# Groups of two picks instead of four in an expert retrieval, v rows added two groups behind

## The reference, cut to what matters

```python
def block(args):
    xb, eb, gb = args
    a = jnp.einsum('td,thkd->thk', xb, u_tab[eb])
    coef = gb.astype(xb.dtype) * jax.nn.gelu(a)
    return jnp.einsum('thk,thkd->td', coef, v_tab[eb])
```

## Time and profile before

| | us |
|---|---|
| median of 3 runs | 2582.67 (2576.73 to 2587.87) |
| the profiled execution | 2576.18 |
| its span, first to last instruction | 2574.3 |
| PE, DVE, ACT, POOL busy | 1894.1, 1692.0, 550.0, 1521.5 |
| HBM read | 936.55 MB, 365 GB/s over the span |

### The profile page before, as it was taken

How to read it: one execution, slowest core, us unless ns; L and a number is a source line. 1 busy time by engine, 2 the same in 40 slices (tenths; PEclk the granted TensorE clock), 3 DMA queues, 4 the chain that set the end, 5 groups by cost and what they waited for, 6 DMA issues and landing times.

```text
span 2574.3 us, 19294 instructions
## 1 busy us (share of the span) xinstructions
PE 1894.1 (74%) x5226; PEld 836.3 (32%) x5226; DVE 1692.0 (66%) x3756; ACT 550.0 (21%) x1369; POOL 1521.5 (59%) x1562
## 2 busy tenths in 40 slices
PE   6779776686777555686677678677777777777776
PEld 3444343352232212343332234335322222222222
DVE  0337876776899555557779657577968886554444
ACT  1432323221122001212222112222211111111111
POOL 2005554666677545566656655466667777677774
PEclk8879987898999767798889988788989999999999
DMA  9918987999999999999899999789999999999997
GB/s 340 347 60 310 405 326 250 382 367 403 386 408 408 402 394 373 341 369 406 327 404 387 366 378 396 284 300 384 360 374 409 409 409 409 373 410 410 409 409 319
DMA packets 295970, 939.88 MB, mean 365 GB/s; under 512 B 30692, under 2 KB 44360, under 8 KB 295864
## 3 DMA queue, kind: packets, MB, share of 16 engines
q0 software_dynamic: 222496, 809.28, 80.9%
q1 hardware_dynamic: 71304, 127.38, 13.5%
q10 hardware_dynamic: 2064, 2.00, 0.2%
HBM read 936.55 MB, written 2.00 MB: 365 GB/s over the span
## 4 chain that ended last, share of the span: by engine, by line
DMA 27%; DVE 23%; PE 20%; POOL 13%; issue 8%; ACT 4%; SPq 1%; DVEq 0%; ACTq 0%; POOLq 0%
DMA vbuf<-in_peer_v_dram,eidx 11%; DVE ubuf L2143 10%; DMA ubuf<-in_peer_u_dram,eidx 10%; PE ysum L1234 7%; POOL vbuf L2200 6%; POOL ubuf L2200 6%; PE bank L948 4%; DMA wring<-in_w_mod_dram 3%; DVE acc L2136 2%; PE bank L1200 2%; PE bank L1167 2%; DMA wring<-in_w_in_dram 1%; SPq L844 1%; DVE scratch L2017 1%; DVE scratch L2019 1%
## 5 line engine op out<-in xcount | busy, mean ns | idle before, releaser
L1234 PE MATMUL ysum<-vbuf,diag 128*128 128x512 f32 x2356 | 1212.9, 649 | 354.3 <-DMA vbuf<-in_peer_v_dram,eidx 253.6
L2143 DVE CUSTOM_DVE_ANT_0 ubuf<-ubuf,h_bank 128x1024 f32<-128x1024 f32 x768 | 910.5, 1219 | 386.4 <-DMA ubuf<-in_peer_u_dram,eidx 358.9
L2200 POOL DMA_INDIRECT ubuf<-in_peer_u_dram,eidx x768 | 737.1, 960 | 601.4 <-DVE dot L2143 245.4
L2200 POOL DMA_INDIRECT vbuf<-in_peer_v_dram,eidx x768 | 771.1, 1004 | 402.6 <-issue 189.9
L1234 PEld LDWEIGHTS ysum<-vbuf,diag 128*128 128x128 f32 x2356 | 440.9, 203 | 1077.9 <-DMA vbuf<-in_peer_v_dram,eidx 585.1
L1620 ACT ACTIVATE act_dot<-dot 128x4 f32<-128x4 f32 x192 | 39.4, 205 | 1259.4 <-DVE dot L2143 1257.9
L2136 DVE SCALAR_TENSOR_TENSOR acc<-vbuf,coef,acc 128x1024 f32<-128x1024 f32 x173 | 222.1, 1284 | 68.4 <-DMA vbuf<-in_peer_v_dram,eidx 56.9
L1631 ACT ACTIVATE diag<-ident,coef 128x128 f32<-128x128 f32 x589 | 201.1, 393 | 255.7 <-DVE coef L2148 203.7
L948 PE MATMUL bank<-wring,hT 128*128 128x512 f32 (+1 forms) x416 | 191.5, 618 | 21.7 <-DMA wring<-in_w_in_dram 12.5
L948 PEld LDWEIGHTS bank<-wring,hT 128*128 128x128 f32 x416 | 84.6, 206 | 124.4 <-issue 98.4
L891 PE MATMUL bank<-wring,cond 128*32 128x512 f32 x288 | 51.8, 855 | 56.8 <-DMA wring<-in_w_mod_dram 50.7
(11 more groups left out here) (287 smaller groups left out, 1332.9 us busy)
## 6 DMA issues: line engine op xcount, KB each, us to landing
wring<-in_w_mod_dram SPq DMA_DIRECT2D x19, 2048.0 KB, 19.4
wring<-in_w_in_dram SPq DMA_DIRECT2D x11, 2048.0 KB, 19.6
wring<-in_w_out_dram SPq DMA_DIRECT2D x7, 2048.0 KB, 19.7
wring<-in_peer_w_q_dram SPq DMA_DIRECT2D x7, 2048.0 KB, 18.9
ubuf<-in_peer_u_dram,eidx POOLq DMA_INDIRECT x768, 9.1
vbuf<-in_peer_v_dram,eidx POOLq DMA_INDIRECT x768, 9.1
wring<-in_w_in_dram SPq DMA_DIRECT2D x4, 1664.0 KB, 16.7
ubuf<-in_w_mod_dram SPq DMA_DIRECT2D x3, 2048.0 KB, 14.4
```

Of the source, the lines that this page charges most:

```text
L1234: mm = pe.matmul(ysum[:, b, :], diag[:, (n - 1) % DIAGS, :], vbuf[:, pick % V_SLOTS, 512 * b:512 * b + 512], start=first and r == rows[0], ...
L2143: dve.tensor_tensor_reduce(ubuf[:, n % U_SLOTS, :], ubuf[:, n % U_SLOTS, :], h2_bank[:, :, :].rearrange("p b n -> p (b n)"), 1.0, 0.0, ALU ...
L2200: pool.indirect_dma_start(buf[:, n % slots, :], None, rows, bass.IndirectOffsetOnAxis(eidx[:, t % 2, p:p + 1], 0))\
```

## The change

Groups have two picks (`G = 2`, so `NG` = 64). The v rows of group i are added beside group i + 2 (`LAG`), on PE and on DVE; a tile ends with two groups of rows. `coef` has three buffers in place of two, as a group's coefficients are still read while the next two are written. The slots of u and v stay at six. The planner's constants for four picks are halved, and its tail is 4 groups in place of 2; the last two groups of a tile have one row of two on DVE.

```diff
-G = 4
-U_SLOTS = G + 2
-V_SLOTS = G + 2
+G = 2
+LAG = 2
+U_SLOTS = 6
+V_SLOTS = 6
-TAIL = 2
+TAIL = 4
-ROW_US, ADD_US, DOTS_US = 2.1, 1.3, 5.4
+ROW_US, ADD_US, DOTS_US = 2.1, 1.3, 2.7
-PACE_US = 9.6
+PACE_US = 4.8
...
     for what, i, *more in schedule():
         if what == "groups":
-            if more[0]:
-                share[i, more[0] - 1] = shares(pe, dve)[1]
+            if more[0] >= LAG:
+                share[i, more[0] - LAG] = shares(pe, dve)[1]
             if more[1] == NG:
-                share[i, more[0]] = 1
+                for k in range(NG - LAG, NG):
+                    share[i, k] = 1
...
-        coef = sb("coef", [P, 2, G])
+        coef = sb("coef", [P, LAG + 1, G])
...
-                if lo <= 1 < hi:
+                if lo <= LAG < hi:
                     if t:
 
                         pe.wait_ge(y_taken, nth("y_taken", t - 1))
                     group(0, True, False)
-                for i in range(max(lo - 1, 1), hi - 1):
+                for i in range(max(lo - LAG, 1), hi - LAG):
                     group(i, False, False)
                 if hi == NG:
-                    group(NG - 1, False, True)
+                    for i in range(NG - LAG, NG):
+                        group(i, False, i == NG - 1)
...
-                    if i:
-                        add_rows(i - 1)
+                    if i >= LAG:
+                        add_rows(i - LAG)
                     dve.wait_ge(gelu_done, NG * t + i + 1)
-                    dve.tensor_tensor(coef[:, i % 2, :], act_dot[:, :], gates[:, t % 2, G * i:G * i + G], ALU.mult).then_inc(coef_done, 1)
+                    dve.tensor_tensor(coef[:, i % (LAG + 1), :], act_dot[:, :], gates[:, t % 2, G * i:G * i + G], ALU.mult).then_inc(coef_done, 1)
...
                 if hi == NG:
-                    add_rows(NG - 1)
+                    for i in range(NG - LAG, NG):
+                        add_rows(i)
...
                 fetch_u(n)
-                if n >= G:
-                    fetch_v(n - G)
-            for n in range(total - G, total):
+                if n >= G * LAG:
+                    fetch_v(n - G * LAG)
+            for n in range(total - G * LAG, total):
                 fetch_v(n)
```

More of the change, by code:

```diff
@@ L1630, in group @@
                             act.wait_ge(v_free, n - DIAGS)
-                        act.activation(diag[:, (n - 1) % DIAGS, :], ident[:, :], ACT.Copy, scale=coef[:, i % 2, r:r + 1]).then_inc(diag_built, 1)
+                        act.activation(diag[:, (n - 1) % DIAGS, :], ident[:, :], ACT.Copy, scale=coef[:, i % (LAG + 1), r:r + 1]).then_inc(diag_built, 1)
                 if lo == 0:
@@ L2132, in add_rows @@
                         if vector_rows(n) - 1 == (vector_rows(PICKS * t - 1) if t else 0):
-                            dve.tensor_scalar(acc[:, :], vbuf[:, n % V_SLOTS, :], coef[:, i % 2, r:r + 1], None, ALU.mult).then_inc(v_added, 1)
+                            dve.tensor_scalar(acc[:, :], vbuf[:, n % V_SLOTS, :], coef[:, i % (LAG + 1), r:r + 1], None, ALU.mult).then_inc(v_added, 1)
                         else:
                             dve.wait_ge(v_added, vector_rows(n) - 1)
-                            dve.scalar_tensor_tensor(out=acc[:, :], in0=vbuf[:, n % V_SLOTS, :], scalar=coef[:, i % 2, r:r + 1], in1=acc[:, :],
+                            dve.scalar_tensor_tensor(out=acc[:, :], in0=vbuf[:, n % V_SLOTS, :], scalar=coef[:, i % (LAG + 1), r:r + 1], in1=acc[:, :],
                                                      op0=ALU.mult, op1=ALU.add).then_inc(v_added, 1)
```

## The result

The changed kernel takes 2574.0 us (median of 19 runs, 2569.6 to 2580.9), the kernel before 2583.9 us beside it (19 runs, 2576.7 to 2590.7). The ratio is 0.9970, with a 95% interval of 0.9961 to 0.9978: about 8 us faster (the two medians differ by 9.9). The forecast was 2608, slower; the range held the time. The profiled execution took 2573.6 us (before 2576.2), so the two profiles themselves differ by less than the medians do, and a reading by stretches can explain the larger shifts within the kernel, not the last few microseconds of the whole.

The account below looks back on a forecast made before the run. DMA bytes were taken to bound the kernel wherever no engine holds picks back. The terms 8 + 11 + 5 + 4 + 5 - 8 gave +25 us, 2601 from the profile's 2576.2; 2608 as median of runs, range 2545 to 2645.

Parts of the forecast that it names:

- What bounds the kernel: Whole kernel: DMA bytes at 410 GB/s wherever no engine holds picks back; 105 us in tiles 0 to 3 winnable.
- Twice the handovers: 192 more gelu and coef handovers, 0.43 us each, cost where DVE sets the pace: +8 us, bounds 0 and 82.
- table loads: ACT: about 10 more table switches at 1.30 us, 13 us, of which 5 show: +5 us (0 to 13).
- Packing of tile 1: Tile 1's top-k: denser gaps make three halves 18 us too long, cushion takes about 7: +11 us.
- Packing of tile 2: Tile 2's top-k: level near 8.2, 3.2 us a pick instead of 3.0, 7 us less the cushion: +5 us.
- Who adds v rows: Projections of tiles 2 and 3: 29 rows move from DVE to PE, mostly covered by DMA: +4 us, bounds 0 and 60.
- Finer interleaving: Two attention stretches: scores come earlier behind two rows than four; -4 us each, -8 in all, bounds -32 and +6 a stretch.
- The lag: Fetch order and lag: POOL's sequence stays the same, and the third coefficient buffer only makes the lag legal: 0 us.
- rival B: Faster: finer PE and DVE alternation shortens attention stretches and starved places, -35 us, 2548; attention share over 0.8 decides; 28%.
- Boundaries: Five tile starts: the last two groups' DVE rows of 1.28 us lie within DVE's 9.9 us wait: 0 (0 to 7).
- the signs for a wrong prediction: Wrong if tile 1 isn't longer, or if tiles 0 and 3 are each over 10 us shorter.
- A: The forecast itself: DVE and PE get tighter, coarser gaps; 2590 to 2640, attention share 0.66 to 0.75; 50%.

Follow-up runs that it names:

- a_places: The changed kernel's groups of two and lag of two, but beats dealt by four picks as in the kernel before, 179 rows on DVE; 2597.3 us, 1.0055.
- f_pairs: The changed kernel with tile 1's modulation beats planned at 3.0 and 0.8 us, so two share a gap; 2557.6 us, 0.9897.
- a_cap: a_places with at most two of four rows on DVE, 133 instead of 179, spread over both pairs; 2586.1 us, 1.0022.
- s_split: a_places with each gap's beats shared between its two pairs, still 179 rows on DVE; 2573.9 us, 0.9968.
- m_dve: The kernel before (groups of four, lag one) with each gap's beats cut in two on DVE alone; 2560.9 us, 0.9913.
- c_lag1: The changed kernel with a lag of one group instead of two, 146 rows on DVE instead of 152; 2572.9 us, 0.9972.
- f_mid: f_pairs with each gap's beats cut in two, a dot behind each half, on PE too; 2545.9 us, 0.9867.
- end0: The changed kernel with no row on DVE in a tile's last two groups, instead of one each; 2566.1 us, 0.9939.
- best: The changed kernel with the edits of f_pairs and end0, and layer 1's constants and keys requested earlier; 2555.9 us, 0.9906.
- m_two: The kernel before with each gap's beats cut in two on DVE, and PE's four rows put between the halves; 2591.9 us, 1.0041.

## Why the prediction was wrong, step by step

**What bounds the kernel** stood. Bytes set the time wherever no engine holds the picks back, POOL has no margin to catch up, and all that moved was time lost against 409 GB/s.

**Twice the handovers, +8, and table loads, +5.** a_places has the handovers with the lag, and the table loads of before (35): 14 us where I had 8. So the handovers, with the lag, were sized too low. The gelu waits were forecast at 2 x 59 and came to 190.8 us, since a gelu queued behind a beat on ACT waits with it. Table loads rose by 8 in the changed kernel, forecast about 10; no run has them by themselves. A load with the activation behind it, in its timeline of ACT:

```profile
1032.28 0.40 ACT L1634 ACTIVATE diag<-ident,coef 128x128 f32<-128x128 f32 x1 [0.23 <-DVE coef L2151]
1032.70 1.28 ACT L1333 ACT_TABLE_LOAD   x1
1034.00 0.52 ACT L1333 ACTIVATE decay<-decay 128x384 f32<-128x384 f32 x1
```

It takes 1.3 us with both sides of it. The drain of 1.38 us that the Trainium skill (ScalarE: Activation LUTs, What ACT_TABLE_LOAD costs) adds doesn't show here either.

**Packing of tile 1, +11.** The mechanism was right and the half searches were as worked out, 56.6 us for 20 picks against 57.3 (64 picks in the 181 us above). The cushion was not: I took 7 of 18 us off for what is queued, and tile 1 got 17 us longer, its ledger 0.2 to 16.6 in the top-k. My reading is that a queue of some 9 us is drawn once and then has to be filled again; no run tests it. Some 5 of the 17 are the handovers, as a_places, dealt as before, loses 4.9 there. f_pairs gives nearly all of it back. DVE was busy 93% of that stretch, not over 95; the 0.27 us for each gelu are idle and were in the sum, but not in the share I named.

**Packing of tile 2, +5.** Top-k there lost 9.9 instead of 6.2 us: +4. It isn't packing: a_places, with its beats at their old places, loses 10.3. The planner's level came to 7.5 and not to the 8.2 that I had worked out.

**Who adds v rows, +4.** 616 rows on PE and 152 on DVE were forecast as 618 and 150, but the sign isn't borne out. PE was busy 78.6 of 84 us in the projection of tile 2, up from 70.7, and the rate fell from 402 to 390 GB/s only, as the term said. Over the kernel the row on DVE was the dearer one: a_cap moved 46 rows to PE, spread the rest, and gained 8 us. A likely reason is that a row of 1.28 us on DVE stands between a dot and the next coefficient, and one of 2.07 on PE stands beside them.

**Finer interleaving, -8: the step that failed.** The prediction had the bounds (-32 a stretch) and took -4 for each of two attention stretches, "near the end at zero because beats depend on each other one by one". What the new dealing does to tiles 0 and 3 it left at nothing, "at equal mean density". Measured from a_places, which has every handover and none of the dealing, the dealing with its 27 rows took 41 us off tiles 0, 2 and 3. 27 of them are in the mixers:

| lost in the mixers, us | tile 0 | tile 2 | tile 3 | longest time between two dots in tile 3's |
|---|---|---|---|---|
| before | 36.3 | 11.8 | 34.9 | 17.8 |
| a_places | 38.4 | 10.0 | 36.8 | 15.5 |
| s_split | 37.8 | 7.6 | 34.6 | 12.2 |
| a_cap | 33.9 | 6.4 | 28.4 | 12.3 |
| the changed kernel | 32.2 | 2.9 | 23.3 | 7.4 |

The density is indeed about that of before (42 picks beside tile 3's mixers instead of 44), so density was the wrong thing to ask for. What differs is how evenly the side work lies: by the planner's numbers a gap in tile 3's mixers has at most 4.5 us of DVE work in the changed kernel, 7.5 in a_places, and 6.5 in s_split, which cuts a gap by the number of its beats.

What carries the gain isn't shown. A dot frees a u slot and POOL has six, so the longest time without a dot is a likely measure, and the last column falls with the loss in the changed kernel. But s_split shortens that time and gains 2 us in tile 3, and a_cap, with fewer rows on DVE, gains 8 there at the same longest time as s_split. m_dve shows only that cutting DVE's spells alone is worth 22 us in the kernel before; its ledger spreads this over tiles 0, 2 and 3 (3.6, 4.5 and 6.0).

**The lag, 0.** I had "the third coefficient buffer only makes the lag legal". In the changed kernel taking it away changed nothing that the time shows (c_lag1, with six DVE rows fewer); in s_split it is worth 61 us, in f_mid 43. I had seen PE's waits for diag, 67.5 us, and used them only as an argument for rival B. The fault was to price each part alone: finer alternation brings PE to its rows earlier, and in s_split and f_mid the lag pays for that. Why the planner's own dealing (c_lag1) needs it so much less than s_split's is not settled; there it costs 18 us in tile 0 and gives about as much back in the others.

**Boundaries, 0 (0 to 7).** end0 gains 8 us over the changed kernel, so the row on DVE at a tile's end wasn't free there. Beside f_pairs (best) the gain is gone.

**The sum.** By the ledger of the profiles: handovers with the lag +18 (a_places; +14 by the times), then the dealing and the rows, +11 in tile 1, -41 in tiles 0, 2 and 3, +5 in tiles 4 and 5. That is -6, where the medians have -10 and the ratio -8. My sum had +8 for handovers, +11 in tile 1, and +6 for everything else (5 + 4 + 5 - 8). So the miss is the 41 us, and handovers sized 10 us too low and the 5 us of tiles 4 and 5 hide a part of it. s_split (-6, -14, +2 in tiles 0, 2 and 3) and a_cap (0, -5, -6) point to parts of it in tiles 0 and 2; most of tile 3's 19 us no run isolates. The 105 us that I called all the change could win goes by the queues' share; by bytes tiles 0 to 3 lose 163 before. Of the signs for a wrong prediction that I had named, tile 1 longer spoke for me, tile 3 over 10 us shorter (14) against, and tile 0 (7.5) didn't reach its mark.

Rival B had the place right and was 26 us too large: its -35 left out tile 1's packing. The attention stretch of tile 3 did what it asked, share 0.85 where 0.8 was to decide; tile 0's came to 0.77, between A and B. Its mechanism, finer alternation of PE and DVE at the same order of beats, isn't confirmed by s_split, which has it and gains next to nothing in these stretches. A's packing was true in tile 1.

## What to carry to other kernels

Where a queue of fetches has few slots and an in-order engine both frees them and does side work, look at the longest spell in which it frees none, and not only at its busy share or the mean density of side work: cutting that spell on this one engine (m_dve), with nothing else changed, was worth 22 us, more than the change of group size with all its parts (8). A consumer with a blocking wait at the head of an in-order queue (PE's rows here) may need its producer an extra group ahead when its own side work is alternated finer: the cut on both engines lost some 11 us without the lag (m_two), and taking the lag from kernels that have the cut lost 61 and 43. And when capacity is halved, go through the planner's gaps: a pair of beats that no longer fits one gap can eat the gain, and don't count on the queue's depth to cover a stretch (it took some 2 of 18 us off here, where I had 7).

## What the runs showed of the hardware that I had not expected

TensorE's mean granted clock was higher in the kernels that give it more v rows, though they are otherwise alike. Spans and mean granted clocks of a_places and of a_cap, which has 46 more rows on PE:

```profile
core 0: 2594.2 us, clock 0.894
```

```profile
core 0: 2582.7 us, clock 0.917
```

The kernel before has 0.892 and the changed one 0.921. All eight kernels with 589 rows on PE have 0.892 to 0.900, all eleven with 616 to 639 rows 0.910 to 0.928. In the projection stretch of tile 2 the clock went from 0.90 to 0.98, with PE busy 78.6 us instead of 70.7; over the kernel a matmul of the projections fell from a mean of 618 to 601 ns. The higher clock doesn't set the time here: m_dve has 0.896 and is faster than the changed kernel. None of these runs moves the clock alone, so why it rises isn't shown.
